# Values projected by token, no turning stage, and the final norm inside the last MLP block

## The chip, the cores and the metric

The kernel runs on one core of a Trainium2 chip. The time is the device time of one launch, in microseconds. Five engines work side by side and meet at semaphores: TensorE (PE; its weight loads are listed as PEld), VectorE (DVE), ScalarE (ACT), GpSimd (POOL) and SyncE (SP), which only issues transfers. TensorE runs at one of two clocks, 1.2 or 2.4 GHz; the granted clock of a stretch is given as a share of the higher one.

## What is computed

One layer of a decoder trunk on 1024 prompt tokens and on 8 sequences of 8 new tokens each, which have 1024 past keys and values in pages of 128. All is float32.

```python
h = rms_norm(x, g_mix) * (1 + sc1) + sh1
q_sb, k_sb, v_sb, q_g, k_g, v_g, r_g, a_low = split_columns(h @ w_in)   # 512 512 512 256 256 512 512 16
o_sb = stick_breaking_attention(q_sb, k_all, v_all, q_offset, b_sb)      # 8 heads of 64
o_g, s_new = gla_chunked(q_g, k_g, v_g, log_a, gla_s0)                   # 4 heads
x = x + ga1 * (concat([o_sb, rms_norm(o_g) * silu(r_g)]) @ w_out)
h2 = rms_norm(x, g_ffn) * (1 + sc2) + sh2
x = x + ga2 * (square(relu(h2 @ w_up)) @ w_down)
y = rms_norm(x, g_final)
```

Outputs are y, the new k and v rows by token, and the gated linear attention's states.

## The kernel before

Activations live transposed, features on partitions and the 1088 tokens (1024 prompt, 64 sample) along the free axis, in three chunks of 384, 384 and 320 (CHUNKS). A float32 product is three matmuls (`three_products`, L389 to L391): each operand is split into a rounded high part and the rest as low part, and high x high, high x low and low x high are summed. The first argument is the stationary one. Weights come in panels of 256 columns, in two buffers: ScalarE rounds the high part, GpSimd subtracts for the low part (`lo_done`).

The stages run one after the other:

- `stage_start`: conditioning, first norm, transposed `hT_hi`, `hT_lo`.
- `stage_project_in` (L394 to L521): q, k, v of the stick-breaking heads and the last 128 columns (with the gate's 16), 13 tiles of 128 features by three chunks, 24 matmuls a group. ScalarE and VectorE copy the banks out in turn, and each tile is stored to the DRAM array `projT`, features by tokens.
- `stage_project_gla_and_sample_attention`: for the 8 sequences in turn, the attention of the new tokens over the cached pages; between its small products lie the remaining 12 tiles of the projection (q, k, v and r of the gated heads), cut into pieces of three matmuls (`dense`, `pieces`), in the order of the table DENSE, one and a half tiles a sequence. A sequence: `turn_weights` of the one before, `score` (per page: turn four blocks of keys, copy them out, multiply), `turn_out`, `values` of the one before, the rest of the pieces. Meanwhile ScalarE and VectorE work the sequence's chain: three activations, a maximum, a scan over 1024 keys (L1087), a subtraction, an exponential (L1008). Key pages have two buffers and are issued by SP, value pages one (`sa_v`) and are issued by GpSimd. Scores and sums over the new keys (L858 to L869) stand ahead of the first sequence.
- `stage_natural`: reads k, v and gated v back from `projT`, turns them to tokens by features (108 transposes), stores k and v as outputs and gated v in the DRAM array `vgnat`; beside it the first q and k of prompt attention are loaded and scaled, and its bias rows and constants filled in (`PairOperands`).
- `stage_prompt_attention`: 48 steps over head pairs and blocks, a pipeline over all engines.
- `stage_gla`: gated linear attention, with the second half of the conditioning.
- `stage_project_out_and_norm`, then `stage_mlp`: eight blocks of 512 hidden features in a hardware loop; 12 groups up, 24 groups down (output tile by output tile, three chunks each), six banks, VectorE adding each down group to `x1T` (L2415).
- `stage_final` (L2460 on): for nine token tiles, 8 transposes, squares with a running sum (L2512), logarithm and exponential for the root, and two products with the gain on VectorE (L2531), a store each.

Of the kernel before, what the change touches and what calls it, by code (L numbers as in the profile page):

```python
# [19 lines left out]
P = 128  # L20
# [149 lines left out]
def stage_start(g, w_in):  # L170
# [10 lines left out]
    with ExitStack() as ctx:  # L181
# [10 lines left out]
        tmp = [sb(f"n1_tmp{i}", [P, 512]) for i in range(3)]  # L192
# [26 lines left out]
        with nc.Block() as block:  # L219
# [41 lines left out]
            def _(act):  # L261
# [19 lines left out]
                for j, (gi, t0, n, k) in enumerate(steps[:NPR]):  # L281
# [3 lines left out]
                    for out, done in ((hT_hi[:, k, t0 * P:t0 * P + 512], s_hi), (tmp[j % 3][:], s_tmp)):  # L285
                        act.activation(out, g.bank[j % NB][:], ACT.Identity, scale=g.mul1[:, k, 0:1], bias=g.mod(SH1, k)).then_inc(done, 1)

            @block.vector
            def _(dve):
# [28 lines left out]
                for j, (gi, t0, n, k) in enumerate(steps):  # L318
                    t = tmp[j % 3]
                    if n > 1:  # L320
                        dve.wait_ge(s_hi, j + 1)
                        dve.wait_ge(s_tmp, j + 1)
                        dve.tensor_tensor(hT_lo[:, k, t0 * P:t0 * P + 512], t[:], hT_hi[:, k, t0 * P:t0 * P + 512],
# [70 lines left out]
def stage_project_in(g, w, hT_hi, hT_lo):  # L394


    nc, io = g.nc, g.io
    w_in = io["w_in"][0]
    NP = ROW_QG // PANEL
    assert NP % 2 == 0  # L400
    with ExitStack() as ctx:
        stg = [g.sb(f"in_stage{i}", [P, T], ctx=ctx) for i in range(4)]
        s_mm = g.sem("in_group_summed")
        s_aev = g.sem("in_act_evacuated")
        s_dev = g.sem("in_dve_evacuated")
        s_out = [g.sem(f"in_stage{i}_stored") for i in range(4)]
        last_w = slice(0, P)
        with nc.Block() as block:
            @block.sync
            def _(sp):  # L410
                with sp.Fori(0, NP // 2 - 1) as n:
                    for s in range(2):
                        sp.wait_ge(w.lo_done, n * 2 + s + 1)
                        w.load(sp, w_in, bass.ds((n * 2 + 2 + s) * PANEL, PANEL), s)
                sp.wait_ge(w.lo_done, NP - 1)
                sp.dma_start(w.raw[0][:, :, last_w], w_in[:, LAST:IN_W].rearrange("(k p) c -> p k c", p=P)).then_inc(w.loaded[0], 16)

            @block.gpsimd
            def _(pool):
                def low(i, s):  # L420
                    pool.wait_ge(w.hi_done, i + 1)
                    pool.tensor_tensor(w.lo[s][:], w.raw[s][:], w.hi[s][:], ALU.subtract).then_inc(w.lo_done, 1)

                with pool.Fori(0, NP // 2 - 1) as n:
                    low(n * 2 + 1, 1)
                    low(n * 2 + 2, 0)
                low(NP - 1, 1)
                pool.wait_ge(w.hi_done, NP + 1)
                pool.tensor_tensor(w.lo[0][:, :, last_w], w.raw[0][:, :, last_w], w.hi[0][:, :, last_w],
                                   ALU.subtract).then_inc(w.lo_done, 1)  # L430

            @block.tensor
            def _(pe):
                pe.sem_inc(s_mm, 12)

                def groups(s, n, tiles):
                    for m in range(tiles):
                        for c, (t0, tw) in enumerate(CHUNKS):
                            gi = m * 3 + c

                            pe.wait_ge(s_dev if gi % 2 else s_aev, n * 6 + s * 3 + gi // 2 + 1)
                            for k in range(KD):
                                cols = slice(m * P, (m + 1) * P)
                                last = three_products(pe, g.bank[gi][:, 0:tw], w.hi[s][:, k, cols], w.lo[s][:, k, cols],
                                                      hT_hi[:, k, t0:t0 + tw], hT_lo[:, k, t0:t0 + tw], k, KD)
                            last.then_inc(s_mm, 1)

                with pe.Fori(0, NP // 2) as n:
                    for s in range(2):
                        pe.wait_ge(w.lo_done, n * 2 + s + 1)  # L450
                        groups(s, n, 2)
# [3 lines left out]
            def evacuate(eng, copy, mine, s_ev, prime):  # L455
                if prime:
                    eng.sem_inc(s_ev, 3)
# [2133 lines left out]
```

## Time and profile before

| | us |
|---|---|
| median of 3 runs | 1911.29 (1909.64 to 1911.66) |
| profiled execution | 1905.86 |
| its span | 1904.3 |
| stage_start | 0 to 73.6 |
| stage_project_in | 73.6 to 232.4 |
| sample attention with gated projection | 232.4 to 529.8 |
| stage_natural | 529.8 to 574.9 |
| prompt attention | 574.9 to 800.8 |
| gated linear attention | 800.8 to 974 |
| output projection and second norm | 974 to 1114 |
| MLP | 1114 to 1877.4 |
| stage_final | 1877.4 to 1904.3 |

TensorE is busy for 1691.6 us of the span, 89%, VectorE for 740.4, ScalarE for 605.2, GpSimd for 438.5; the mean granted clock is 0.93. A timeline row gives start, duration, engine, line, operation, what is written from what, shapes and a count, and in brackets how long the engine sat idle before and what ended that. Matmuls are pipelined: the distance between starts is what one costs, its duration is longer.

### The profile page before, as it was taken

What the parts mean: (1) busy time and instruction counts of PE and PEld (TensorE: products, weight loads), DVE (VectorE), ACT (ScalarE), POOL (GpSimd) and SP (SyncE); (2) the same over time, 40 slices, a digit from 0 to 9 for tenths busy, and PEclk for the clock granted to TensorE, in tenths of its full rate; (3) what the DMA queues carried; (4) which work ended last, traced back from release to release, by engine and by line L of the source; (5) the groups of instructions that cost most, each with busy time, mean ns of one, the idle gap of its engine ahead of it and who ended that gap; (6) DMA issues with size and microseconds to landing.
All of it is one profiled execution on the core that took longest, in us unless ns stands there. A gap on an engine that the chain in (4) does not pass through costs nothing. (4 is left out here: it accounts for less than half of the span.)

```text
span 1904.3 us, 27580 instructions
## 1 busy us (share of the span) xinstructions
PE 1691.6 (89%) x10652; PEld 1474.9 (77%) x10652; DVE 740.4 (39%) x1269; ACT 605.2 (32%) x1130; POOL 438.5 (23%) x310
## 2 busy tenths in 40 slices
PE   4799879999748888887749989999999999999996
PEld 2699867777644444445649979999999999999995
DVE  3300033434226777555831563232323232323234
ACT  4411022322117877534523542121211111111113
POOL 1011122122110000100134543333323232323220
PEclk9799979999968999858879999999999999999998
DMA  8121156653380000184163221111111111111102
GB/s 316 56 92 58 54 159 211 190 179 113 125 308 18 23 23 1 56 241 161 61 207 107 93 67 45 44 44 44 44 44 44 44 44 44 44 44 44 44 0 105
DMA packets 119253, 173.39 MB, mean 91 GB/s; under 512 B 7626, under 2 KB 80669, under 8 KB 119174
## 3 DMA queue, kind: packets, MB, share of 16 engines
q1 hardware_dynamic: 110464, 142.10, 22.7%
q0 software_dynamic: 5120, 16.78, 2.8%
q10 hardware_dynamic: 3590, 13.48, 1.7%
q8 instruction: 48, 0.79, 0.2%
q14 instruction: 31, 0.25, 0.0%
HBM read 146.57 MB, written 25.76 MB: 90 GB/s over the span
## 5 line engine op out<-in xcount | busy, mean ns | idle before, releaser
L389 PE MATMUL psum<-op_hi,out_hi 128*128 128x384 f32 (+1 forms) x960 | 320.3, 334 | 3.7 <-DVEq L2387 1.9
L391 PE MATMUL psum<-op_hi,out_lo 128*128 128x384 f32 (+1 forms) x960 | 314.2, 327 | 0.0
L390 PE MATMUL psum<-op_lo,out_hi 128*128 128x384 f32 (+1 forms) x960 | 314.1, 327 | 0.0
L391 PE MATMUL psum<-mlp_a_hi,out_lo 128*128 128x384 f32 (+1 forms) x768 | 250.9, 327 | 0.0
L390 PE MATMUL psum<-mlp_a_lo,out_hi 128*128 128x384 f32 (+1 forms) x768 | 250.6, 326 | 0.0
L389 PE MATMUL psum<-mlp_a_hi,out_hi 128*128 128x384 f32 (+1 forms) x768 | 250.4, 326 | 0.0
L2337 POOL TENSOR_TENSOR out_lo<-out_raw,out_hi 128x2048 fp32r<-128x2048 f32 x31 | 143.2, 4619 | 271.7 <-ACT out_hi L2360 271.7
L2400 DVE TENSOR_TENSOR mlp_sq<-mlp_relu 128x384 f32<-128x384 f32 (+1 forms) x96 | 88.3, 921 | 280.0 <-ACT mlp_relu L2375 280.0
L389 PEld LDWEIGHTS psum<-op_hi,out_hi 128*128 128x128 f32 x960 | 181.4, 189 | 8.0 <-DVEq L2387 2.9
L390 PEld LDWEIGHTS psum<-op_lo,out_hi 128*128 128x128 f32 x960 | 181.2, 189 | 2.5
L391 PEld LDWEIGHTS psum<-op_hi,out_lo 128*128 128x128 f32 x960 | 181.1, 189 | 0.0
L2415 DVE SCALAR_TENSOR_TENSOR x1T<-psum,modT,x1T 128x384 f32<-128x384 f32 (+1 forms) x192 | 108.9, 570 | 158.2 <-PE psum L391 158.2
L2360 ACT CAST out_hi<-out_raw 128x2048 fp32r<-128x2048 f32 x31 | 59.1, 1908 | 295.9 <-PE psum L391 295.9
L389 PEld LDWEIGHTS psum<-mlp_a_hi,out_hi 128*128 128x128 f32 x768 | 144.2, 188 | 0.0
L391 PEld LDWEIGHTS psum<-mlp_a_hi,out_lo 128*128 128x128 f32 x768 | 144.2, 188 | 0.0
L390 PEld LDWEIGHTS psum<-mlp_a_lo,out_hi 128*128 128x128 f32 x768 | 144.1, 188 | 0.0
L2344 POOL TENSOR_TENSOR mlp_a_lo<-mlp_sq,mlp_a_hi 128x384 fp32r<-128x384 f32 (+1 forms) x96 | 92.8, 974 | 207.5 <-ACT mlp_a_hi L2367 207.5
L2375 ACT ACTIVATE mlp_relu<-psum 128x384 f32<-128x384 f32 (+1 forms) x96 | 45.5, 474 | 266.1 <-PE psum L391 266.1
L389 PE MATMUL psum<-op_hi,pg_hi 128*128 128x384 f32 (+1 forms) x288 | 106.7, 371 | 0.0
L389 PE MATMUL psum<-op_hi,in_hi 128*128 128x384 f32 (+1 forms) x312 | 102.6, 329 | 3.9 <-ACTq L483 3.9
L391 PE MATMUL psum<-op_hi,in_lo 128*128 128x384 f32 (+1 forms) x312 | 102.3, 328 | 0.0
L390 PE MATMUL psum<-op_lo,in_hi 128*128 128x384 f32 (+1 forms) x312 | 102.3, 328 | 0.0
(316 smaller groups left out, 2839.8 us busy)
## 6 DMA issues: line engine op xcount, KB each, us to landing
sa_k<-in_cache_k SPq DMA_DIRECT2D x64, 256.0 KB, 3.2
sa_v<-in_cache_v POOLq DMA_DIRECT2D x64, 256.0 KB, 3.9
out_raw<-in_w_up SPq DMA_DIRECT2D x16, 1024.0 KB, 5.2
out_raw<-in_w_down SPq DMA_DIRECT2D x16, 1024.0 KB, 5.0
out_raw<-in_w_out SPq DMA_DIRECT2D x12, 1024.0 KB, 5.2
ada_w<-in_w_ada SPq DMA_DIRECT2D x22, 512.0 KB
ada_w<-in_w_ada SPq DMA_DIRECT2D x4, 2048.0 KB, 15.4
projT<-in_stage ACTq DMA_DIRECT2D x12, 544.0 KB, 2.7
```

The source lines that it names most:

```text
L389: pe.matmul(out, w_hi, x_hi, start=(k == 0), stop=False)
L390: pe.matmul(out, w_hi, x_lo, start=False, stop=False)
L391: return pe.matmul(out, w_lo, x_hi, start=False, stop=(k == nk - 1))
L2337: pool.tensor_tensor(w.lo[s][:], w.raw[s][:], w.hi[s][:], ALU.subtract).then_inc(w.lo_done, 1)
L2344: pool.tensor_tensor(a_lo[:, m, t0:t0 + tw], q[i % 3][:, 0:tw], a_hi[:, m, t0:t0 + tw], ALU.subtract).then_inc(s_al, 1)
L2360: act.copy(w.hi[s][:], w.raw[s][:]).then_inc(w.hi_done, 1)
L2375: act.activation(r[i % 3][:, 0:tw], g.bank[i % NBANK][:, 0:tw], ACT.Relu).then_inc(s_re, 1)
L2400: dve.tensor_tensor(q[i % 3][:, 0:tw], r[i % 3][:, 0:tw], r[i % 3][:, 0:tw], ALU.mult).then_inc(s_sq, 1)
L2415: dve.scalar_tensor_tensor(out=out, in0=b[:, 0:pw], scalar=g.mod(GA2, kc), in1=out, op0=ALU.mult, op1=ALU.add).then_inc(s_dn, 1)
```

## The change

In `stage_project_in`, q, k and the last tile stay as they are; v and gated v are now projected by token: the 128 tokens of a tile are the stationary operand and the panel's 256 columns the moving one, nine token tiles a panel, so that they come out as tokens by features and are stored so (v as output, gated v in `vgnat`, in halves). k's tiles are turned out of their staging buffers in 12 turns between the groups that follow. The loops are written out. All stores are issued by SP.

`stage_natural` is gone. In the sample stage the eight tiles left (q, k and r of the gated heads) go one to a sequence, with one piece a page in `score` and two a page in `values`. The scores over the new keys stand behind the first page of the first sequence, their sums behind the first chunk of pieces after it, and value pages have two buffers. The new v rows are read by token. Stores are issued by SP. Prompt attention's constants are made at this stage's end, by GpSimd.

Prompt attention loads its first q and k, then v (from the output), then the second q and k at its own start, and zeroes and fills the bias rows there, and splits the sample's attention output.

In the MLP the first seven blocks stay in the loop. In the last one, the down groups go chunk by chunk, on four banks, and the final norm of the token tiles of a finished chunk is set among the groups of the next (`turned_at`, `summed_at`, `scaled_at`); the last three tiles follow after the last group. Gain and outputs use the weights' raw buffers, so that VectorE waits for the last low part ahead of its first addition. In `stage_start` one temporary shares a buffer.

```diff
 def stage_project_in(g, w, hT_hi, hT_lo):
+    PANELS = [(ROW_Q, PANEL), (ROW_Q + PANEL, PANEL), (ROW_K, PANEL), (ROW_K + PANEL, PANEL), (LAST, P),
+              (ROW_V, PANEL), (ROW_V + PANEL, PANEL), (ROW_VG, PANEL), (ROW_VG + PANEL, PANEL)]
+    NP, AP, V0 = len(PANELS), 4, 5
+    NB = 6
+    groups = [(p, m, c) for p in range(AP) for m in range(2) for c in range(3)] + [(AP, 0, c) for c in range(3)]
+    groups += [(p, tt, 0) for p in range(V0, NP) for tt in range(N9)]
+    turns = [(f, b) for f in range(4, 8) for b in range(3)]
...
+                        if j < NF:
+                            last = three_products(pe, bank[:, 0:tw], w.hi[p % 2][:, k, cols], w.lo[p % 2][:, k, cols],
+                                                  hT_hi[:, k, t0:t0 + tw], hT_lo[:, k, t0:t0 + tw], k, KD)
+                        else:
+                            n = P if m < NT else TS
+                            toks = slice(m * P, m * P + n)
+                            last = three_products(pe, bank[0:n, 0:PANEL], hT_hi[:, k, toks], hT_lo[:, k, toks],
+                                                  w.hi[p % 2][:, k, :], w.lo[p % 2][:, k, :], k, KD)
+                    last.then_inc(s_mm, 1)
+                    u = (j - feature_end(4)) - 1
+                    if 0 <= u < NU:
+                        turn(u)
...
+                evacuated(sp, len(groups))
+                store_tokens(g.vgnat[0:TP, PANEL:], g.vgnat[TP:T, PANEL:], vst[1][:, :, PANEL:])
...
-def stage_natural(g, pairs):
...
-def stage_project_gla_and_sample_attention(g):
+def stage_project_gla_and_sample_attention(g, prompt):
-    DENSE = [[[(0, 0), (0, 1)], [(0, 2), (1, 0)]], [[(1, 1), (1, 2)], [(2, 0), (2, 1), (2, 2)]]]
+    TILES = [ROW_QG + i * P for i in range((ROW_VG - ROW_QG) // P)] + [ROW_RG + i * P for i in range((ROW_A - ROW_RG) // P)]
+    assert len(TILES) == NSEQ
-        vpg = sb("sa_v", [P, NPAGE, SB])
+        vpg = [sb(f"sa_v{i}", [P, NPAGE, SB]) for i in range(2)]
...
                     for j in range(NPAGE + 1):
+                        if j == 1 and s == 0:
+                            pe.wait_ge(s_cd, 7)
+                            bias_scores()
+                            new_scores()
...
-                            pieces(between, 2)
+                            pieces(between, 1)
...
-                        pieces(between, 3)
+                        pieces(between, 2)
...
+                for s in range(NSEQ):
+                    if s > 0:
+                        turn_weights(s - 1)
+                    first = dense(s, [0])
+                    score(s, first)
+                    pieces(first, KD + 1)
+                    chunks = dense(s, [1, 2])
+                    if s == 0:
+                        pieces(chunks, KD)
+                        new_sums()
+                    if s > 1:
+                        turn_out(s - 2, s % 2)
+                    if s > 0:
+                        values(s - 1, (s - 1) % 2, chunks)
+                    pieces(chunks, 2 * KD + 1)
...
 def stage_prompt_attention(g, ops):
             def _(sp):
+                ops.load(sp, 0, 0)
+                ops.load_values(sp)
+                ops.load(sp, 1, 1)
             def _(pool):
-                for p in range(2, NPAIR):
+                pool.memset(ops.bias[:].bitcast(F32), 0.0).then_inc(ops.s_bz, 1)
+                for p in range(NPAIR):
                     ops.scale(pool, p, p % 2)
...
-def stage_mlp(g, w, h_hi, h_lo, n2):
+def stage_mlp_and_final(g, w, h_hi, h_lo, n2):
+        LASTD = [(c, m) for c in range(3) for m in range(KD)]
+        def fin_bank(t, half):
+            return g.bank[half if t == NT else 4 + 2 * (t % 2) + half]
+        def turned_at(c, m):
+            return 3 * (c - 1) + m // 2 - 1 if c > 0 and m in (2, 4, 6) else None
+        def summed_at(c, m):
+            return 3 * (c - 1) + m // 2 - 1 if c > 0 and m in (3, 5, 7) else None
+        def scaled_at(c, m):
+            return 3 * (c - 1) + m // 2 - 2 if c > 0 and m in (4, 6) else 3 * (c - 1) + 2 if c > 0 and m == 7 else None
...
+                up(NG - 1)
+                dve.wait_ge(s_g, 16)
+                dve.wait_ge(w.lo_done, 4 * NG)
+                for i, (c, m) in enumerate(LASTD):
+                    add(NG - 1, i, m, c, g.bank[i % 4])
+                    if summed_at(c, m) is not None:
+                        summed(summed_at(c, m))
+                    if scaled_at(c, m) is not None:
+                        scaled(scaled_at(c, m))
...
+                    if c == 0 and m % 4 == 0:
+                        pe.wait_ge(w.lo_done, n * 4 + d + 3)
+                    t = turned_at(c, m)
+                    if t is not None:
+                        pe.wait_ge(s_dn, NDN + n * NDN + c * KD)
+                        if t < 2:
+                            pe.wait_ge(s_re, n * NUP + NUP)
+                        turn(t)
+                pe.wait_ge(s_dn, NDN + n * NDN + NDN)
+                for t in range(6, N9):
+                    turn(t)
...
-def stage_final(g):
```

## Rows read from the trace of the kernel before

**Rows 1.** Windows view by stage: busy and count of PE, PEld, DVE, ACT, POOL, clock, DMA.
```profile
73.60:232.40 158.80, 155.99 (x936) 155.73 (x936) 10.20 (x19) 19.82 (x26) 25.46 (x6) 0.99 0.20 73
232.40:529.80 297.40, 269.87 (x2329) 210.40 (x2329) 105.39 (x134) 70.81 (x88) 69.91 (x89) 0.93 0.50 159
529.80:574.90 45.10, 17.72 (x108) 16.66 (x108) 12.50 (x21) 8.00 (x14) 5.67 (x17) 0.66 0.92 343
...
1877.40:1904.30 26.90, 11.24 (x72) 8.55 (x72) 13.36 (x27) 14.96 (x54) 0.00 (x0) 0.79 0.50 186
```

**Rows 2.** PE's timeline: first matmuls of a 384-, a 320-, a 384-column group.
```profile
103.16 0.33 PE L389 MATMUL psum<-op_hi,in_hi 128*128 128x384 f32 x1
...
107.32 0.31 PE L389 MATMUL psum<-op_hi,in_hi 128*128 128x320 f32 x1
...
110.83 0.34 PE L389 MATMUL psum<-op_hi,in_hi 128*128 128x384 f32 x1
```

**Rows 3.** PE's timeline in prompt attention: back-to-back matmuls of 128, then 256 columns.
```profile
635.16 0.28 PE L1261 MATMUL psum<-pa_sh,pa_pick 128*128 128x128 f32 x1
635.27 0.28 PE L1263 MATMUL psum<-pa_sl,pa_pick 128*128 128x128 f32 x1
...
639.04 0.28 PE L1263 MATMUL psum<-pa_sl,pa_pick 128*128 128x256 f32 x1
639.16 0.28 PE L1261 MATMUL psum<-pa_sh,pa_pick 128*128 128x256 f32 x1
```

**Rows 4.** PE's timeline in the sample stage: two key pages and what lies between.
```profile
388.42 0.60 PE L888 MATMUL psum<-ident,sa_k 128*128 128x128 f32 x4
388.77 0.43 PE L389 MATMUL psum<-op_hi,pg_hi 128*128 128x384 f32 x1
...
390.38 0.66 PE L888 MATMUL psum<-ident,sa_k 128*128 128x128 f32 x4
```

**Rows 5.** PE's timeline over two sequences: weights turned (L902), scores done (L909).
```profile
385.01 1.03 PE L902 MATMUL psum<-ident,sa_a 128*128 128x128 f32 x8
...
402.57 0.33 PE L909 MATMUL psum<-ident,sa_out_rows 128*128 128x128 f32 x1
...
414.78 1.09 PE L902 MATMUL psum<-ident,sa_a 128*128 128x128 f32 x8
...
431.45 0.33 PE L909 MATMUL psum<-ident,sa_out_rows 128*128 128x128 f32 x1
...
448.38 1.03 PE L902 MATMUL psum<-ident,sa_a 128*128 128x128 f32 x8
```

**Rows 6.** ScalarE's timeline: last step of the attention's chain in the first of them.
```profile
412.76 1.06 ACT L1008 ACTIVATE sa_a<-sa_a 128x1024 f32<-128x1024 f32 x1 [5.91 <-DVE sa_a L1089]
```

**Rows 7.** Timeline of the first sequence: key pages issued, first turn, its weights turned.
```profile
238.72 0.47 SPq L766 DMA_DIRECT2D sa_k<-in_cache_k  x1
...
255.56 1.11 PE L888 MATMUL psum<-ident,sa_k 128*128 128x128 f32 x4
...
285.17 1.92 PE L902 MATMUL psum<-ident,sa_a 128*128 128x128 f32 x8 [3.36 <-ACT sa_a L1008]
```

**Rows 8.** PE's timeline in the last sequence: the products with v.
```profile
523.62 3.64 PE L928 MATMUL psum<-sa_v,sa_w 128*32 128x128 f32 x64 [9.42 <-DMA sa_v<-in_cache_v]
```

**Rows 9.** DMA issues: engine, count, KB each, median us from issue to landing.
```profile
in_raw<-in_w_in SPq DMA_DIRECT2D x6, 1024.0 KB, 5.2
...
gl_k<-projT SPq DMA_DIRECT2D x1, 1088.0 KB, 5.1
```

**Rows 10.** GpSimd's timeline in the last MLP block: its last weights' low part.
```profile
1831.94 4.62 POOL L2337 TENSOR_TENSOR out_lo<-out_raw,out_hi 128x2048 fp32r<-128x2048 f32 x1 [0.76 <-ACT out_hi L2360]
```

**Rows 11.** Timeline of the final norm: the last tile's squares and its output.
```profile
1897.25 0.57 ACT L2512 ACTIVATE fin_sq<-psum 64x512 f32<-64x512 f32 x1
...
1898.29 0.19 ACT L2512 ACTIVATION_READ_ACCUMULATOR fin_sq<-psum 64x1 f32 x1
...
1899.44 1.40 DVE L2531 SCALAR_TENSOR_TENSOR fin_y<-psum,fin_rstd,fin_gain 64x512 f32<-64x512 f32 x2 [0.60 <-ACT fin_rstd L2517]
```

More of the change, by code:

```diff
@@ new lines, in turn @@
+                def turn(u):
+                    f, b = turns[u]
+                    if u >= 2:
+                        pe.wait_ge(s_kc[u % 2], u // 2)
+                    if b == 0:
+                        evacuated(pe, feature_end(f))
+                    for i in range(4 * b, min(4 * b + 4, N9)):
+                        m = P if i < NT else TS
+                        last = pe.transpose(g.bank[NB + u % 2][0:m, (i - 4 * b) * P:(i - 4 * b + 1) * P], stg[f % 4][:, i * P:i * P + m], g.ident[:])
+                    last.then_inc(s_kt, 1)
@@ L524, with split @@
+                starts = {panel_end(p - 2) if p >= 2 else 0: p for p in range(1, NP)}
+                def split(j):
+                    if j in starts:
+                        round_hi(starts[j])
+                group, k_turn = evacuate(act, act.copy, 0)
+                in_order(0, group, k_turn, split)
 class PairOperands:
@@ L848, in _ @@
+                for s in range(1, NSEQ):
+                    low(s)
+                    v_pages(s)
+                prompt.constants(pool)
             @block.tensor
             def _(pe):
-                pe.wait_ge(s_in, 64)
-                for m in range(4):
-                    last = pe.transpose(O[0:TS, m * P:(m + 1) * P], vnewT[:, m, :], g.ident[:])
-                last.then_inc(s_vn, 1)
-                pe.wait_ge(s_c, 10)
-                pe.wait_ge(s_cd, 8)
-                bias = brow[:].rearrange("o j h q -> o (j h q)")
@@ new lines, in score, with bias_scores @@
+                def score(s, between):
+                    slot = s % 2
+                    at_least(pe, s_x, s)
+                    pe.wait_ge(s_k[slot], s // 2 * 128 + 128)
+                    def bias_scores():
+                        for half in range(2):
+                            pe.matmul(Z[:, half * 512:half * 512 + 512], bst[:].rearrange("o p c -> o (p c)"), ones, start=True, stop=False,
+                                      skip_group_check=True)
+                    for j in range(NPAGE + 1):
+                        if j == 1 and s == 0:
+                            pe.wait_ge(s_cd, 7)
+                            bias_scores()
+                            new_scores()
+                        elif j == 0 and s > 0:
+                            bias_scores()
@@ L2519, in _ @@
[L2519 to L2532 removed]
+                n = NG - 1
```

786 lines of the change are left out of this document (373 added, 413 removed).

## The prediction

> **What bounds the kernel now.** I read the windows by stage first, then TensorE's timeline inside each stage that the change touches, then the other engines where TensorE waits. The stage rows show where time can be had at all [rows 1]. The first projection is 158.8 us with 936 matmuls and no gap: it is nothing but products, so it costs what its matmuls cost. The sample stage is 297.4 us with TensorE busy for 269.9. The turning stage is 45.1 us with 17.7 us of TensorE work and a DMA share of 0.92: it is bound by loading what was stored just before and storing it again, and no other stage runs beside it. The final norm is 26.9 us with nothing beside it. The MLP before it has no gap, so work leaves it only if it leaves TensorE.
>
> **Price of a product.** A group of 24 matmuls of 384 columns takes 4.16 us, one of 320 columns 3.51 us [rows 2]; a tile of 128 features (two of the first, one of the second) is 11.83 us. By token the moving side is 256 columns wide, a width that these stages don't show. Prompt attention has it: two such matmuls start 0.12 us apart, two of 128 columns 0.11 us [rows 3]. The line through 384 and 320 columns gives 0.119 for 256, so 256 columns are still bound by the stream and 128 by the load of weights. I take 0.120, with 0.115 to 0.13 as ends.
>
> **Step 1, first projection.** Before: 13 tiles, 153.8 us, and 5.0 around them, 158.8. After: q, k and the last tile are 9 tiles by feature, 106.5. v and gated v are four panels of nine token tiles, 4 x 9 x 24 = 864 matmuls, 103.7 at 0.120 (99 to 112); the ninth tile holds 64 tokens and costs a whole one. By feature the same two matrices are 8 tiles, 94.6, so the order itself loses 9. k is still turned, 36 transposes, now between the products: four transposes are 0.35 us until the next product starts [rows 4] and about 0.1 more to get back to its pace, so 8 turns of four and 4 of one are 4.6. Copies and stores lie under the products (a token group lasts 2.9 us and a copy about 0.5); if that cover were gone, each late copy would stop TensorE only after six banks. The queue of SP now waits for evacuations ahead of later weight loads; a panel lasts 25 us and a 1 MB load lands in 5.2 [rows 9], so nothing waits behind it. At the end the last store is 1.1 MB where it was 68 KB: 3.6 us more before the next stage. Sum 106.5 + 103.7 + 4.6 + 5.0 + 3.6 = 223.4, **64.6 more**.
>
> **Step 2, sample stage.** Four of the twelve feature tiles have left it, one tile and not one and a half goes with each sequence. In the even sequence of the rows, turned weights to scored is 17.56 us with 16 pieces of 384 columns (three matmuls, 0.52 each), the odd one 16.67 with 8 of 384 and 8 of 320 (0.44 each): 9.2 and 9.0 without the pieces [rows 5]. One page is 1.96 [rows 4], 0.92 without its two pieces. From scored to the next turned weights it is 12.21 with 16 pieces (7.67) and 16.93 with 24 (11.83): 4.5 and 5.1 without [rows 5]. After the change each sequence has 8 pieces in the first part, 9.1 + 4.2 = 13.3, and 16 in the second, cut in eight places as in the odd one, 5.1 + 7.7 = 12.8. The period is 26.1. What is late next: the sequence's own chain over ScalarE and VectorE, from scored (402.57) to the end of its last step (413.82), 11.25 [rows 6], still 1.5 under the second part. Seven periods were 4 x 33.6 + 3 x 29.8 = 223.8 and become 182.7: 41.1 less (ends: 26 less, if the period stays at the shorter one of today, 29.8; 47 less, if the extra interruptions are free).
>
> The head: today the first key pages are asked for at 238.72 and first turned at 255.56, because the sums over the new keys stand ahead of them [rows 7]. They now stand behind the first page. Eight page issues and a landing are some 10 us, and two fewer DMAs stand ahead, so I put the first turn 8.6 us earlier (ends 0 and 12). The first sequence was 29.6 from there to its turned weights [rows 7]. It loses 8 pieces (4.2) and takes in the new keys' scores (4.4, as long as they lasted alone on a cold clock) and, under its chain, their softplus and sums, for which the scan waits: 31.8, 2.2 more (ends -4 and +9). The tail: in the last sequence the products with v wait 9.42 us for its pages, which can't be asked for before the sequence ahead has left the one v buffer [rows 8]. With two buffers they are there: 9.4 less, nothing else near. Sum -41.1 - 8.6 + 2.2 - 9.4 = **56.9 less**.
>
> **Step 3, turning stage.** All 45.1 us go [rows 1]. What it hid comes out: the first q and k of prompt attention are asked for at the stage's start. 1.1 MB out of the same array lands in 5.1 [rows 9]; with the second issue, the scaling on GpSimd (about 1.0) and semaphores I take 7.5 to the first score (6 to 12). The zeroing and filling of the bias rows, about 4 us on GpSimd and VectorE, lies beside the load. v, 2 MB, is queued behind them and is needed some 12 us after the first score; were it late, only the first multiplication waits. The clock is at its low level at this point in both kernels. **37.6 less**.
>
> **Step 4, last block and final norm.** The down products keep their number. Turning six of nine token tiles among them costs 8 transposes each, about 0.9: 5.4 more. The last weights' low part is ready at 1836.56 [rows 10], and the new order reaches them after four groups, at 1828.39 + 8.32 = 1836.71: no wait. But VectorE now waits for them before its first addition, and with four banks in place of six TensorE waits for that addition, 0.6. Behind that wait on VectorE stand only the additions; nobody else needs them. The norm's work on tiles 0 to 5 lies under products of 1.8 to 2.1 us a group; an output costs VectorE 1.4 [rows 11], which one addition (0.6) beside it still allows. After the last product, 28.2 us remain today (1876.1 to 1904.3). Then: last addition 1.0, turned and squared tile 6 by 3.1, tile 7 (its banks wait for tile 5's output) by 5.2, its logarithm and root 0.6, tile 8's squares 1.23 [rows 11] and root by 8.2, the last two outputs one behind the other to 10.5, and 3.4 for the last store as today: 13.9 (12.5 to 17). -14.3 + 5.4 + 0.6 = **8.3 less**.
>
> **Sum.** 64.6 - 56.9 - 37.6 - 8.3 = -38.2. The profiled execution is 1905.9 (span 1904.3) and would be 1867.7; the median of the timed runs is 5.4 above it, 1911.3, and becomes **1873.1**.
>
> **Rivals.** (a) The period of a sequence stays at 29.8, because transfers or the chain end it: 5.1 MB in 26 us is 197 GB/s, with the SP and GpSimd queues issuing sixteen pages in it. For it: the margin over the chain is thin. Against: TensorE has no gap in these sequences today, and the rows show what fills them. Price 7 x 3.7 = 26: 1899. (b) The load of weights sets the pace by token. The stage rows show the load path busy for 155.7 us with 936 loads, 0.166 each [rows 1]; at that pace 864 matmuls are 143.4, 40 more, and the time is 1913, no change. Against: starts 0.12 and 0.11 apart [rows 3]. (c) The other side: the load isn't hidden at all at this width. Then a matmul costs its stream and its load, 0.12 + 0.11 = 0.23, 864 of them 198.7, 95 more: 1968, slower. It decides from a spacing of 0.164 on (38.2 / 864 above 0.120). Against it, 384 columns come at 0.173 [rows 2], 0.11 less than their stream and a load together. The Trainium skill, TensorE: Matmul & The Clock Gate, section "The mechanism" of Part 3, says that a load overlaps matmuls in flight only when its row group differs, which all these full-height matmuls fail; by that rule the outcome is this rival's. The trace disagrees with it at 384 and at 256 columns. (d) The clock falls in the scored part, where a page keeps one piece of dense work instead of two. At 1.2 GHz for half of it, seven sequences gain 46 us: 1919, slower. Against: the stage holds 0.93 today, transposes included [rows 1], with no gap to lower it. The same page, "Part 4: PE-mode transpose", says that transposes don't count as work for the clock; that rule would lead here, and no row shows it.
>
> **How the numbers follow.** The forecast, 0.81: 1873, alone 1855 to 1893 (projection +8 / -5, sample stage +15 / -10, heads and tails +6 / -5, not all at once). (a) 0.09, at 1899; (b) 0.04; (c) 0.02; (d) 0.04. The range 1853 to 1894 leaves out the rivals. A change of 0.2%, 3.8 us, is about what a measurement of this kernel can tell from none. Faster: forecast, (a) and a part of (d), 0.91. Same: most of (b), 0.04. Slower: (c), most of (d), the rest of (b), 0.05.
>
> **What would show it.** Right: token matmuls 0.12 apart; first projection near 223; turned weights 26 apart in the sample stage, with no wait for v at its end; 7 to 8 us from that stage's end to the first score; 14 us after the last product. Wrong: starts of 0.15 or more by token; a gap on TensorE between scored and turned; a granted clock under 0.9 between the first and the last sequence; waits of the additions on ScalarE's roots in the last block.

## The result and the profile after

The changed kernel takes **1864.5 us** (median of four runs, 1858.8 to 1864.9), the kernel before 1910.5 (median of four runs beside it, 1909.4 to 1911.7): ratio 0.974, 95% interval 0.972 to 0.977. The profiled execution has a span of 1863.2 where the one of before has 1904.3, 41.1 less. The forecast was 38.2 less on that scale, and 1873.1 for the median.

Two lines of the page of the changed kernel: busy time by engine, and TensorE's granted clock in 40 slices.

```profile
PE 1682.8 (90%) x10864; PEld 1463.4 (79%) x10864; DVE 731.7 (39%) x1261; ACT 605.2 (32%) x1132; POOL 438.3 (24%) x307
...
PEclk8699997999989999767879999999999999999999
```

TensorE's busy time fell by 8.8 us; the other 32 of the 41.1 were idle time. Where they went, the windows view of the changed kernel by stage says (columns as in rows 1: start:end, length, busy time and count of PE, PEld, DVE, ACT and POOL, clock, DMA share, GB/s):

```profile
77.20:298.30 221.10, 215.41 (x1548) 214.84 (x1548) 17.47 (x37) 29.98 (x46) 34.70 (x8) 0.99 0.25 82
298.30:534.60 236.30, 216.81 (x2037) 156.02 (x2037) 99.18 (x122) 67.15 (x84) 63.16 (x98) 0.94 0.59 182
534.60:540.60 6.00, 0.01 (x2) 0.05 (x2) 4.56 (x8) 0.00 (x0) 1.96 (x2) 0.69 0.81 259
...
1850.10:1863.20 13.10, 3.06 (x25) 2.56 (x24) 6.80 (x15) 5.42 (x20) 0.00 (x0) 0.79 0.49 182
```

These are the first projection, the sample stage, the wait ahead of the first score (all that is left in the place of the turning stage) and the stretch behind the last product. The table goes by the instructions' own times, so a tenth can differ from the windows:

| stretch | before | after | change | forecast |
|---|---|---|---|---|
| start to first product | 73.6 | 77.2 | +3.6 | 0 |
| first projection | 158.8 | 221.1 | +62.3 | +64.6 |
| sample stage | 297.4 | 236.2 | -61.2 | -56.9 |
| turning stage, then first score | 45.1 | 6.0 | -39.1 | -37.6 |
| first score to first turn of x (untouched) | 405.1 | 407.3 | +2.2 | 0 |
| to the last block's last weights (untouched) | 851.8 | 852.2 | +0.4 | 0 |
| from there to the last product | 44.2 | 50.0 | +5.8 | +6.0 |
| behind the last product | 28.2 | 13.1 | -15.1 | -14.3 |
| sum | | | **-41.1** | **-38.2** |

**Projection.** TensorE's timeline (start, duration, engine, line, operation, tiles and shape; in brackets the idle time ahead and what ended it): two token matmuls in a row of a whole tile, two of the ninth tile (64 tokens), and a turn of k between products.

```profile
250.50 0.28 PE L389 MATMUL psum<-in_hi,op_hi 128*128 128x256 f32 x1
250.61 0.28 PE L390 MATMUL psum<-in_lo,op_hi 128*128 128x256 f32 x1
...
290.50 0.28 PE L390 MATMUL psum<-in_lo,op_hi 128*64 128x256 f32 x1
290.62 0.28 PE L391 MATMUL psum<-in_hi,op_lo 128*64 128x256 f32 x1
...
190.28 0.60 PE L502 MATMUL psum<-ident,in_stage 128*128 128x128 f32 x4
190.64 0.36 PE L389 MATMUL psum<-in_hi,op_hi 128*128 128x256 f32 x1
```

Starts by token are 0.118 apart, and 0.117 in the ninth tile; 864 of them are the 101.8 us from 190.6 to 292.5. A turn of four delays the next product by 0.36.

**Sample stage.** An even sequence, as in rows 5: weights turned (L891), scores done (L898), the chain's first and last step on ScalarE, and the next turned weights.

```profile
372.12 1.04 PE L891 MATMUL psum<-ident,sa_a 128*128 128x128 f32 x8
...
385.35 0.33 PE L898 MATMUL psum<-ident,sa_out_rows 128*128 128x128 f32 x1
385.49 1.02 ACT L967 ACTIVATE sa_a<-psum 128x1024 f32<-128x1024 f32 x1 [2.13 <-PE psum L884]
...
389.72 2.40 POOL L820 TENSOR_TENSOR pg_lo<-pg_raw,pg_hi 128x1024 fp32r<-128x1024 f32 x1 [7.22 <-ACT pg_hi L1009]
389.99 4.28 DVE L1065 TENSOR_TENSOR_SCAN sa_later<-sa_a,sa_new_sums 128x1024 f32<-128x1024 f32 x1
...
395.56 1.06 ACT L1004 ACTIVATE sa_a<-sa_a 128x1024 f32<-128x1024 f32 x1 [5.92 <-DVE sa_a L1067]
```

The turned weights stand at 346.45, 372.12, 398.00 and so on to 527.38: seven periods are 180.9 us, and from the second on they are 25.88 each, without a gap. The first part is 13.2, the second 12.65, the chain ends 11.3 behind the scores: it has 1.4 of room. In the last sequence the products with v stand at 529.76 without a wait, where rows 8 had 9.42. At the stage's head the first key page is turned 16.2 behind the start (23.2 in rows 7), at the end of this chain of issues (SPq, with the idle time of TensorE in the last row):

```profile
298.34 0.26 SPq L757 DMA_DIRECT2D sa_table<-in_page_table  x1
...
302.48 8.57 SPq L752 DMA_DIRECT2D sa_k<-in_cache_k  x8
...
314.52 1.12 PE L877 MATMUL psum<-ident,sa_k 128*128 128x128 f32 x4 [21.87 <-DMA sa_k<-in_cache_k]
```

**Ahead of the first score**, the scaling of q on GpSimd (in brackets its wait for the load) and the first score:

```profile
539.40 1.04 POOL L635 TENSOR_SCALAR pa_q<-pa_q 128x1024 f32<-128x1024 f32 x1 [3.88 <-DMA pa_k<-projT]
540.59 0.80 PE L1207 MATMUL psum<-pa_q,pa_k 64*128 64x128 f32 x4 [7.75 <-POOL pa_q L635]
```

**Last block.** VectorE's additions wait for the last weights' low part (L2373, GpSimd) for 7.09, TensorE for the first addition only 0.5 behind it. A token tile turned among the products lasts 1.03, but the next product starts 0.79 behind its start (1820.19 to 1820.98). Behind the last product the last norm needs two waits of TensorE, 0.97 and 0.98, and one store:

```profile
1804.79 2.19 DVE L2483 SCALAR_TENSOR_TENSOR x1T<-psum,modT,x1T 128x384 f32<-128x384 f32 x4 [7.09 <-POOL out_lo L2373]
...
1820.19 1.03 PE L2572 MATMUL psum<-ident,x1T 128*128 128x128 f32 x8
1820.98 0.42 PE L389 MATMUL psum<-mlp_a_hi,out_hi 128*128 128x384 f32 x1
...
1851.08 1.09 PE L2572 MATMUL psum<-ident,x1T 128*128 128x128 f32 x8 [0.97 <-DVE x1T L2483]
1853.15 1.97 PE L2572 MATMUL psum<-ident,x1T 128*128 128x128 f32 x16 [0.98 <-DVE out_raw L2498]
1859.88 0.50 SPq L2351 DMA_DIRECT2D y_sample<-out_raw  x1
```

### The profile page after: what moved, and what is told of

Same layout as the page of the kernel before. It is cut to its first block and busy times, and to the rows that moved or that the text cites. A ratio compares the mean times of both kernels' runs of the same rounds, so it can differ in the third digit from the quotient of the medians.

```text
span 1863.2 us, 27708 instructions
## 1 busy us (share of the span) xinstructions
PE 1682.8 (90%) x10864; PEld 1463.4 (79%) x10864; DVE 731.7 (39%) x1261; ACT 605.2 (32%) x1132; POOL 438.3 (24%) x307
## 5 line engine op out<-in xcount | busy, mean ns | idle before, releaser
L2373 POOL TENSOR_TENSOR out_lo<-out_raw,out_hi 128x2048 fp32r<-128x2048 f32 x31 | 143.1, 4617 | 271.8 <-ACT out_hi L2396 271.8
L389 PE MATMUL psum<-in_hi,op_hi 128*128 128x256 f32 (+1 forms) x288 | 80.7, 280 | 0.0
L391 PE MATMUL psum<-in_hi,op_lo 128*128 128x256 f32 (+1 forms) x288 | 80.4, 279 | 0.0
L390 PE MATMUL psum<-in_lo,op_hi 128*128 128x256 f32 (+1 forms) x288 | 80.3, 279 | 0.0
L389 PE MATMUL psum<-op_hi,pg_hi 128*128 128x384 f32 (+1 forms) x192 | 75.7, 394 | 0.0
```

Of the source, the lines that this page charges most:

```text
L389: pe.matmul(out, w_hi, x_hi, start=(k == 0), stop=False)
L390: pe.matmul(out, w_hi, x_lo, start=False, stop=False)
L391: return pe.matmul(out, w_lo, x_hi, start=False, stop=(k == nk - 1))
```

## The experiments

All start from the changed kernel but two, which say so. Its time is 1864.5, or 1866.8 where it ran beside the experiment. None leaves out work.

### Half as wide by token

```
-for k in range(KD):
-    last = three_products(pe, bank[0:n, 0:PANEL], ..., w.hi[p % 2][:, k, :], w.lo[p % 2][:, k, :], k, KD)
+for h in range(2):
+    cols = slice(h * P, (h + 1) * P)
+    for k in range(KD):
+        last = three_products(pe, bank[0:n, cols], ..., w.hi[p % 2][:, k, cols], w.lo[p % 2][:, k, cols], k, KD)
```

> The changed kernel, but each product by token is cut in two of 128 columns: 1728 matmuls with 1728 weight loads where there were 864 of each, the same number of columns streamed. Nothing is left out. Load hidden but with a pace of its own (the forecast's reading of the 128-column starts 0.11 apart): 1728 x 0.11 = 190 us where 864 x 0.118 = 102 stood, so 88 us more, about 1953. If only the streamed columns cost (0.06 for 128): no change, 1865. If the load is not hidden at all (rival c, 0.06 + 0.11 = 0.17 each): 294, 192 more, about 2056.

1944.2 us, 79.7 more; the projection is 301.4 instead of 221.1, 80.3 more. TensorE's timeline, a whole tile and the ninth:

```profile
300.07 0.28 PE L390 MATMUL psum<-in_lo,op_hi 128*128 128x128 f32 x1
300.19 0.27 PE L391 MATMUL psum<-in_hi,op_lo 128*128 128x128 f32 x1
...
366.49 0.22 PE L389 MATMUL psum<-in_hi,op_hi 128*64 128x128 f32 x1
366.55 0.22 PE L390 MATMUL psum<-in_lo,op_hi 128*64 128x128 f32 x1
```

The load is hidden and has a pace of its own, 0.112 on average for 128 columns of weights; where the stationary side has 64 the starts are 0.060 apart. So 1536 x 0.1117 + 192 x 0.0605 = 183.2, where 864 x 0.1177 = 101.7 stood: 81.5. The products by feature ahead of them were 1.0 shorter, since the clock came up 3.3 us behind the first product and not 5.7. That makes 80.5, where the stretch grew by 80.3. The expected 88 priced the ninth tile like the others. For a whole tile, the stream of 128 columns alone (0.06) and load plus stream (0.17) are both excluded. At 64 columns the load can't be told from the stream: the line through 0.173, 0.146 and 0.118 for 384, 320 and 256 moving columns gives 0.063 for 128, so 0.060 only says that the load of 64 costs no more. The Trainium skill, TensorE: Matmul & The Clock Gate, section "LDWEIGHTS (loading the stationary operand)", has a load cost its columns over 1.2, in ns: 107 and 53. The trace agrees for 128, with 5 ns more, and doesn't contradict it for 64.

### The dense pieces moved out from under the chain

```
-first = dense(s, [0])            # and one piece a page
+first = dense(s, [0, 1])         # from s = 1 on, two pieces a page
 score(s, first)
-chunks = dense(s, [1, 2])
+chunks = dense(s, [2])
```

> The changed kernel, but from the second sequence on 16 pieces of dense work stand in the scored part and 8 under the chain, where it was 8 and 16. TensorE's work is the same. The forecast says that a sequence is the first part plus the longer of TensorE's second part and the chain: the first part becomes 13.2 + 4.2 = 17.4, TensorE's second part 12.7 - 4.2 = 8.5, and the chain's 11.1 to 11.5 takes over, so the period goes from 25.9 to 28.7 or a little more: 7 x 2.8 = 20 us more, about 1884, with gaps on TensorE of 2.5 to 3 us before each turned block. If the sequence is bound by TensorE's sum alone (the chain has room wherever the pieces stand): no change, 1865. If the four gaps-free parts are bound by transfers (rival a), no change either, and the period stays 25.9.

1895.2 us, 30.7 more. The seven periods are 213.1 instead of 180.9, 30.4 each. TensorE's timeline, two of the turned weights, and the windows view of the 10 us behind each of the six that waited 2.7 to 2.9:

```profile
401.59 1.97 PE L891 MATMUL psum<-ident,sa_a 128*128 128x128 f32 x8 [2.70 <-ACT sa_a L1004]
...
464.42 1.09 PE L891 MATMUL psum<-ident,sa_a 128*128 128x128 f32 x8 [2.70 <-ACT sa_a L1004]
```

```profile
369.86:379.86 10.00, 10.00 (x52) 8.22 (x56) 1.39 (x2) 1.76 (x3) 3.20 (x6) 0.66 0.92 296
401.59:411.59 10.00, 10.00 (x56) 8.17 (x56) 1.38 (x2) 1.76 (x3) 3.23 (x6) 0.67 0.88 301
433.27:443.27 10.00, 10.00 (x59) 8.08 (x60) 1.38 (x2) 1.76 (x3) 3.23 (x6) 0.72 0.92 302
464.42:474.42 10.00, 10.00 (x65) 8.47 (x66) 1.93 (x3) 1.76 (x3) 3.23 (x6) 0.83 0.89 299
494.72:504.72 10.00, 10.00 (x59) 8.08 (x60) 1.39 (x2) 1.76 (x3) 3.23 (x6) 0.72 0.80 248
525.96:535.96 10.00, 10.00 (x65) 8.46 (x66) 1.99 (x3) 1.76 (x3) 5.48 (x19) 0.83 0.76 247
```

The wait for the chain is 2.7, as expected: a sequence is its first part plus the longer of the second part and the chain. That explains periods of 28.7 (the last, with a wait of only 0.81, 26.8), 199.0 for the seven. The other 14.1 is the clock: it fell to its low level at every one of the six waits or up to 2 us behind it, with a granted clock of 0.66 to 0.83 over the next 10 us, and each of the six periods that start there is 1.5 to 3.0 longer than its sum. In three of the six it had fallen before the turned weights, and their eight transposes take 1.97 where they take 1.04 without a wait; in the other three it fell among or behind them, and they take 1.09 to 1.34. The same stretch of the changed kernel (398 to 408) has 1.00. So a gap of 2.7 on TensorE cost its own length and 1.5 to 3.0 more.

### The same, with GpSimd out of the scan's way

This starts from the kernel with the pieces moved.

```
 def low(i):
     pool.wait_ge(s_hi, i + 1)
+    at_least(pool, s_x, i)
     pool.tensor_tensor(wlo[i % 2][:], raw[i % 2][:], whi[i % 2][:], ALU.subtract)...
```

> The previous experiment with the dense pieces moved (16 in the scored part, 8 under the chain; 1895.2 us, periods of 30.4 on average, TensorE waits 2.7 for the chain in each), and one more edit: GpSimd makes the low part of the next weights only when the chain of the sequence has left VectorE, so that no GpSimd work stands beside the scan. If a GpSimd operation beside it is what makes the scan last 4.27 us and not the 2.35 of the first and the last sequence: the chain is 1.9 shorter, the wait for it 0.8, the period 28.3 as the last one there already is, 6 x 2 = 12 us less, about 1882. If the scan is long for another reason (its data, its operands): no change, 1895. If the later low part now makes TensorE wait at the start of each sequence, the gain is that much smaller, with a gap in front of the first dense piece.

1871.6 us, 23.6 less than the one before it, twice what was expected. VectorE's timeline has every scan at 2.35, and TensorE waits 0.81 (1.03 the first time):

```profile
390.18 2.35 DVE L1066 TENSOR_TENSOR_SCAN sa_later<-sa_a,sa_new_sums 128x1024 f32<-128x1024 f32 x1
...
394.93 1.09 PE L892 MATMUL psum<-ident,sa_a 128*128 128x128 f32 x8 [0.81 <-ACT sa_a L1005]
```

In the changed kernel the scan starts 0.27 behind the start of GpSimd's operation and ends 2.15 behind its end, almost its own length: it stands still until GpSimd has finished. With the wait down to 0.8 the clock stays up too: the granted clock is 1.00 over all seven periods of 26.8, with the same pieces in the same places, so it was the gap that lowered it. In the traces the seven periods are 25.5 less, 11.4 by the six shorter waits and 14.1 by the clock. The Trainium skill, SBUF — State Buffer, section "SBUF: two separate sides", says that a VectorE operation with two inputs in SBUF and a GpSimd operation hold a shared pair of ports one after the other, for a whole instruction; the trace agrees. In the changed kernel itself this stall costs nothing, since the chain has 1.4 of room.

### One buffer for v

```
-vpg = [sb(f"sa_v{i}", [P, NPAGE, SB]) for i in range(2)]
+vpg = [sb("sa_v", [P, NPAGE, SB])] * 2
...
-    at_least(pool, s_pv, s - 1)
+    at_least(pool, s_pv, s)
```

The low part of the next weights is made ahead of the wait for the buffer, as in the kernel before.

> The changed kernel with one buffer for the pages of v in the sample stage in place of two; the low part of the next weights is made ahead of the wait for the buffer, as in the kernel before. The forecast's reason: only the last sequence pays, its products with v wait about 9.4 us for their pages and the periods stay 25.9, so 9 to 11 us more, about 1874. If the pages are late in each sequence (eight issues on GpSimd's queue and a landing behind the products): a few us in each of seven, 20 or more, 1885 or more. If the second buffer brought nothing: 1865.

1874.8 us, 10.3 more. The periods stay at 25.88. The last sequence:

```profile
539.07 3.64 PE L919 MATMUL psum<-sa_v,sa_w 128*32 128x128 f32 x64 [9.93 <-DMA sa_v<-in_cache_v]
```

A wait of 9.93, and behind it the 64 products take 3.64 where they took 1.95, at a granted clock of 0.50: again the clock behind a gap. Together 11.6, which is what the stretch from the last turned weights to the first score grew by (13.2 to 24.9). The second buffer is worth its 10 us at one place.

### The last block as it was

```
-    stage_mlp_and_final(g, w_mlp, g.op_hi, g.op_lo, n2)
+    stage_mlp(g, w_mlp, g.op_hi, g.op_lo, n2)     # both as in the kernel before
+stage_final(g)
```

> The changed kernel with the last MLP block and the final norm as they were before the change. The forecast priced this part alone at 8.3 us; the two traces say -15.1 behind the last product and +6.2 ahead of it, 8.9. So 8.5 to 9 us more, about 1873.5, with 28.2 us from the last product to the end. If the part only gained because of what the other parts left behind (clock, queues), less than 5 us more: under 1869. If its turns cost nothing among the products, 14 or more: 1879.

1873.3 us, 8.8 more. From the last weights' low part to the end it is 72.4 (72.3 in the kernel before), and 63.1 in the changed one: 9.3. The opposite edit, the new last block in the kernel before (`stage_mlp_and_final` in the place of `stage_mlp` and `stage_final` there, and nothing else):

> The kernel before, with only the last MLP block and the final norm of the changed one: the turns of six token tiles among the last products, the norm under them. The forecast gave 8.3 less for this part and the undoing of it in the changed kernel gave 8.9 more. If the part stands by itself, 8.5 to 9.3 less than before, about 1901.5, with 13.1 from the last product to the end. If it depends on the other parts: less than 5.

1901.1 us against 1911.3, ratio 0.9948 (0.9929 to 0.9968), 10.2 less with 6 to 14 as its interval; the same stretch is 63.2. The part stands by itself, at 9.2 to 9.3.

### The turns of k twice

```
-for i in range(4 * b, min(4 * b + 4, N9)):
+for i in 2 * list(range(4 * b, min(4 * b + 4, N9))):
```

> The changed kernel with every turn of k among the projection's products made twice (72 transposes in place of 36, the same result). The forecast priced the 36 at 4.6 us, 0.45 for four and the way back to the pace of the products. If that holds: 4.6 more, about 1869. If the transposes fill gaps that are there anyway: under 1 us. If each switch between products and transposes is what costs, and not the transposes: under 2 us, since the number of switches is the same. If the clock doesn't count them and falls: 10 or more, with a granted clock under 0.99 between 150 and 200.

1870.0 us, 5.4 more. From first product to last store it is 220.1, and 216.0 to 216.4 in the four kernels with single turns and the same projection whose first product also stood at 77: 3.9 more. TensorE's timeline of a doubled turn and the next product:

```profile
194.30 1.04 PE L502 MATMUL psum<-ident,in_stage 128*128 128x128 f32 x8
195.10 0.36 PE L389 MATMUL psum<-in_hi,op_hi 128*128 128x256 f32 x1
```

The next product starts 0.79 behind the start of eight transposes and 0.36 behind that of four; it is 0.14 and 0.03 for two and one. 8 x 0.43 + 4 x 0.11 = 3.9, the whole difference: a transpose costs 0.11. The way back to the pace of the products, 0.08 to 0.09 once a turn in either kernel, stands beside that. The granted clock stays at 1.00.

### The low part of the first weights on VectorE

```
-w_in.first_lo(pool)
...
+if 0 < j < 5:
+    part = slice(2 * j - 2, 2 * j)
+    done = dve.tensor_tensor(w_in.lo[0][:, part], w_in.raw[0][:, part], w_in.hi[0][:, part], ALU.subtract)
```

> The changed kernel, but the low part of the first weights of the first projection is made by VectorE in four pieces of 512 columns between its steps of the first norm, where GpSimd made it in one operation of 4.5 us. The first product stands at 77.2 in the changed kernel's trace and at 73.6 in the one before; in four traces of kernels that are alike up to there it is 77.0 to 77.3 where VectorE's first operation after the modulation (L166) starts behind GpSimd's and lasts 3.5 to 3.7 us, and 73.8 where it starts 0.8 ahead of it and lasts 0.23. If VectorE is held up by GpSimd's operation beside it: no operation of 3.5 us any more, in no run, the first product at 73 or a little earlier, 3 to 4 us less than a run of 77.2, about 1861. If the two placements are something else (a late transfer, code): the long operation is still there in some runs and the time stays at 1864.5.

1863.0 us: the median can't tell it from the changed kernel. The timelines can. The changed kernel, then the one of half-wide products (whose start is the same program), then this one:

```profile
42.87 4.52 POOL L136 TENSOR_TENSOR in_lo<-in_raw,in_hi 128x2048 fp32r<-128x2048 f32 x1 [38.80 <-ACT in_hi L132]
44.00 3.48 DVE L166 SCALAR_TENSOR_TENSOR mul<-modT,vecT 128x72 f32<-128x72 f32 x1
```

```profile
42.17 0.23 DVE L166 SCALAR_TENSOR_TENSOR mul<-modT,vecT 128x72 f32<-128x72 f32 x1
44.32 4.30 DVE L323 TENSOR_TENSOR op_lo<-n_tmp,op_hi 128x512 fp32r<-128x512 f32 x2 [1.91 <-ACT n_tmp L286]
```

```profile
44.86 0.23 DVE L166 SCALAR_TENSOR_TENSOR mul<-modT,vecT 128x72 f32<-128x72 f32 x1
```

An operation of 0.23 that starts behind GpSimd's ends with it, 3.48 later; where it comes first, the next one with two inputs in SBUF is held instead (GpSimd's runs from 42.95 to 47.46 there). From L166 to the first product it is 33.2, 31.6 and 30.4 in the three. So the hold is real and worth 1.2 to 2.8 us. But L166 itself starts anywhere from 42.0 to 44.9 in thirteen traces, and in all eight that start it at 43.7 or later TensorE's clock is at 0.50 to 0.67 between 30 and 40, in four of the other five at 1.00. Here it was 44.9, so the first product stood at 75.2 and not at 73, and 2.0 of the expected 3 to 4 less than 77.2 are left.

### Another head of the sample stage, and three small edits together

```
+sp.dma_start(g.table[:], io["page_table"]...)            # in the stage before
...
-k_pages(0, 0)
+load_pages(sp, io["cache_k"], kpg[0], 0, s_k[0], range(5, NPAGE))
...
+load_pages(act, io["cache_k"], kpg[0], 0, s_k[0], range(5))
```

> The changed kernel with another head of the sample stage: the page table is loaded in the stage before, five of the first eight key pages are issued by ScalarE's queue and three by SP's, and the low part of the stage's first weights is made by VectorE and not GpSimd. In the changed kernel TensorE waits from the stage's start (298.3) to 314.5 for the first key pages: 4.1 until the first of them is issued, 8.6 for eight issues on one queue, 3.4 to the landing. Issued in 5.3 from the start and landed by 9: first turn some 7 us earlier; the rows for the scores (VectorE, 311.1 today, of which 2.8 is one stalled operation) follow at about 11 from the start and would hold the second step up by 1 to 2. In sum 5 to 7 less, about 1858.5. If the pages are bound by their transfer (2 MB) and not by their issue: under 2 us less.

1863.0 us, only 1.5 less. VectorE also makes the low part of this stage's first weights here, in lines that the excerpt doesn't show. By stretches the edit did most of what it should: last store to first turn 16.7 (19.9 to 21.0 in nine executions with the old head), first turn to turned weights 31.1 (31.5 to 32.1 there), together 4 to 5 less where 5 to 7 were expected.

```profile
299.51 4.70 ACTq L753 DMA_DIRECT2D sa_k<-in_cache_k  x5
...
302.41 3.06 SPq L753 DMA_DIRECT2D sa_k<-in_cache_k  x3
...
310.46 1.12 PE L876 MATMUL psum<-ident,sa_k 128*128 128x128 f32 x4 [17.56 <-DMA sa_k<-in_cache_k]
```

But the untouched stretch from the first score to the first turn of x took 411.6 in this execution and 407.3 in the changed kernel's. To see through that, the changed kernel ran again beside a version with this head, the weights' low part on VectorE and the last store cut:

```
-store_tokens(g.vgnat[0:TP, PANEL:], g.vgnat[TP:T, PANEL:], vst[1][:, :, PANEL:])
+for n0 in (0, 4):
+    evacuated(sp, first + n0 + 4)
+    sp.dma_start(g.vgnat[n0 * P:(n0 + 4) * P, PANEL:]..., vst[1][:, n0:n0 + 4, PANEL:])
+sp.dma_start(g.vgnat[TP:T, PANEL:], vst[1][0:TS, NT, PANEL:])
```

> The changed kernel itself, beside the next one on the same chip, so that a difference of a few us can be told. In ten traces the stretch from the first score of prompt attention to the first turn of x, which no edit touches, lasts 405.1 to 411.6 us, and the first product stands at 73.6 to 78.0; so a median of 1858 to 1867 is expected, and a difference of two kernels under 3 us can't be told from their medians, but can from the stretches themselves.

> The changed kernel with three small edits together: the head of the sample stage of the last experiment, the low part of the first weights on VectorE, and the projection's last store (the last quarter of gated v) cut in three, so that only 64 rows of it are stored behind the last product. By stages: head 4.1 to the first turn and 0.7 behind it (as measured), first product 1.3 to 3 earlier against a run of the same kind, last store: the next stage starts 5.2 us behind the last store's issue today, with 64 rows behind the products about 2.5 to 3 (a small load of this kernel lands in about 2): 2.5 less. In sum 8 to 10 less than the kernel beside it, about 1855.5. If the gains of the small edits are only moved to another wait: under 3 less.

1866.8 us (ratio to before 0.976, 0.974 to 0.979) and **1857.8 us** (0.971, 0.969 to 0.974): 9.0 less, as expected, and the fastest of all. The next stage starts 2.4 behind the last store instead of 4.8, and the first key page is turned 14.3 behind it instead of 19.9. Its profiled execution was the slowest of its six, with a span of 1863.3: prompt attention, which nobody touched, took 277.5 from its first score to the GLA stage's first matmul of q with k (269.4 to 274.2 in the twelve others). The windows view of its second 40 us, then the same of the changed kernel:

```profile
572.70:612.70 40.00, 34.58 (x171) 19.55 (x173) 26.73 (x50) 27.83 (x60) 1.05 (x1) 0.87 0.08 27
```

```profile
580.60:620.60 40.00, 34.81 (x185) 19.34 (x186) 28.58 (x54) 30.20 (x66) 1.05 (x1) 0.96 0.08 27
```

TensorE is not dense there (35 of 40 us), and its clock dips more in one execution than in another. Over the whole stretch the granted clock is 0.86 here and 0.89 in the changed kernel, and the thirteen traces line up by it: 269.4 to 271.7 at 0.88 to 0.89, 273.4 and 274.2 at 0.88, 277.5 at 0.86. Why it dips in one execution more than in another isn't shown.

## Why the prediction was right, step by step

**Price of a token matmul**, 0.120: measured 0.118. Rivals (b) (0.166) and (c) (0.23) are out by the spacing itself. The experiment at half the width shows why 256 columns are the safe side: the load's pace is 0.112, just under the 0.118 of 256 columns. By token costs 101.8, by feature 94.6: the order itself loses 7.

**Step 1**, +64.6 forecast, +62.3 measured. Less by 2.0 for the price (864 x 0.0023), by 0.6 for the turns (4.0 for 4.6: the delays above and the way back to the pace), and by 0.8 for the last store (2.8 and not 3.6 longer until the next stage); more by 1.1 because the clock stayed low for 5.7 us behind the first product, and for 3.5 in the kernel before, which the sum left out.

**Step 2**, -56.9 forecast, -61.2 measured. First part 13.2 (13.3), second 12.65 (12.8), period 25.88 (26.1): right, and the reason is shown by moving the pieces, which made the chain the bound. The term that was mis-sized is the seven periods of the kernel before. The sum took three of them at 29.8 and four at 33.6, 223.8 together; by the first turned weights (285.17) and the last (511.8) they are 226.6. The first of them is 36.46, behind the wait of 3.36 that rows 7 show, and the windows view has the clock down in it:

```profile
285.17:321.63 36.46, 36.46 (x298) 29.06 (x299) 12.06 (x12) 9.03 (x11) 5.16 (x7) 0.91 0.62 207
```

The changed kernel has no wait there and 1.00. With 180.9 for the new periods (182.7) the gain is 45.7 instead of 41.1.

The head gained 7.0 (8.6): from the first page's issue to the first turn it was 12.0 and not some 10, the eight issues alone being 8.6. The first sequence cost 2.3 (2.2), but that agreement is in part luck: the granted clock was 0.78 over its 31.9 us and 0.90 over the 29.6 of before. The tail gained 10.9 (9.4): without the wait the clock stays up and the products with v take 1.95, not the 3.64 of rows 8, a part of the price of that wait which the sum left out.

Rival (a), a period of 29.8, needed the chain to be longer than 12.65, and with GpSimd's operation beside the scan it is 11.3, or the pages to come late, and TensorE is busy for all 180.9 us of the seven periods. Rival (d), a falling clock from the transposes, is out: from the turned weights at 398.00 to the next ones, with 41 transposes among some 250 matmuls, the windows view has

```profile
398.00:423.88 25.88, 25.88 (x254) 18.51 (x251) 12.08 (x14) 8.09 (x10) 6.71 (x9) 1.00 0.68 205
```

What lowered it in the experiments was a gap.

**Step 3**, -37.6 forecast, -39.1 measured: 6.0 to the first score and not 7.5, since 0.5 MB of k landed in 4.5 (median of its loads) and not in the 5.1 of a 1.1 MB load. In the second execution of the changed kernel and in the one with three small edits that median was 5.8 and the first score came 8.6 and 8.3 behind the stage's start, so the 7.5 lies inside what the chip does. The values needed no wait. This step has no experiment of its own: it rests on the two traces.

**Step 4**, -8.3 forecast, -9.3 measured, and the same from both directions. Ahead of the last product +5.8 (+6.0): the addition's wait was 0.5, and the six turns took the rest, 0.9 each as forecast. Behind it 13.1 and not 13.9.

**Where the forecast of the median was off.** 1873.1 against 1864.5: 2.9 is the sum above, 5.4 is what the forecast put between a profiled execution and the median of the runs, and 0.3 is what the new median lies below its profiled execution. The profiled execution of the kernel before (1905.9) was a fast one of its kind (1905.5 to 1917.9 in all runs), that of the changed kernel (1864.9) the slowest of its four. An offset read from one execution was noise.

**What was not foreseen** are the +3.6 at the start and the +2.2 from prompt attention on. Nothing shows that the change made them: the first product stands at 73.8 to 73.9 or at 77 to 78 in kernels whose start is the same program, and with the start of the kernel before it stands at 73.6 in one trace and at 77.4 in the other (the one with the new last block only). The second stretch varies from 405.1 to 415.3 over the thirteen traces.

## What to carry to other kernels

With fp32 operands split in two, a matmul of 256 moving columns already hides its weight load, so the side that a later stage wants can be chosen cheaply (here 101.8 us against 94.6, a thirteenth more); at 128 columns it is the load that is paid. Where TensorE is filled up by pieces of other work, put the pieces under the dependent chain: a gap of 2.7 us there cost its length and then 1.5 to 3.0 more by the clock, one of 0.8 only its length. An edit worth a few us is judged by the stretch that it changes, since the untouched rest of a 1.9 ms kernel moves by more.

## What the chip did that was not expected

- Each of six gaps of 2.7 to 2.9 us on TensorE was followed by a granted clock of 0.66 to 0.83 over the next 10 us, three of them by transposes at 1.97 instead of 1.04. After the seven gaps of 0.8 to 1.0 in the next experiment the clock stayed at 1.00.
- A VectorE operation with two inputs in SBUF that starts beside a GpSimd tensor operation ends its own length after GpSimd's: the scan 4.28 instead of 2.35, an operation of 0.23 3.48.
- With 128 moving columns and a new stationary tile each, starts are 0.112 apart for a stationary tile of 128 columns and 0.060 for one of 64.
- The same program comes to its first product at 73.8 or at 77 to 78, which goes with whether VectorE or GpSimd starts first and with TensorE's clock in the first 40 us.
